# Sparse attention's pairs: the inverse of the sums on VectorE, narrow pairs in one bank, a later turn

## The reference, cut to what matters

```
p_sel = masked_softmax(q @ k_sel.T, pos <= t)
p_win = masked_softmax(q @ k_win.T, pos <= t)
o = gate0 * o_cmp + gate1 * (p_sel @ v_sel) + gate2 * (p_win @ v_win)
masked_softmax(s) = exp(s - max(s)) / sum(exp(s - max(s)))
```

## Time and profile before

| | |
|---|---|
| median of three runs | 1748.11 us |
| the profiled execution's own time | 1748.23 us |
| its span, first to last instruction | 1746.4 us |
| busy: PE / DVE / ACT / POOL | 98% / 56% / 47% / 55% of the span |
| the stage, first maximum to the last product of the values | 1034.1 to 1179.0 us, 8% of the span |

### The profile page before, as it was taken

The page is one execution under the profiler, slowest core; times in us unless marked ns, Lnnn a source line. Parts: engine busy times, 40 slices in busy tenths (PEclk is TensorE's granted clock), DMA queues, the critical chain, the costliest instruction groups (busy, mean ns, idle before and its releaser), DMA issues.

```text
span 1746.4 us, 27720 instructions
## 1 busy us (share of the span) xinstructions
PE 1712.6 (98%) x10482; PEld 1522.1 (87%) x10482; DVE 970.9 (56%) x1638; ACT 825.4 (47%) x1667; POOL 966.7 (55%) x703
## 2 busy tenths in 40 slices
PE   8999999999999999999999999999999999999998
PEld 6988887888888998999888978888988889989996
DVE  4345664244438871586058469984333498428832
ACT  4224553232335552455256358874533556426642
POOL 4544332235444874677446459982842468638862
PEclk9999999999999999999999999999999999999999
DMA  6422122123351433233435330012531223323331
GB/s 226 119 76 60 49 73 58 49 61 98 113 169 49 121 115 115 73 97 116 127 91 148 97 107 3 6 33 73 169 109 61 77 69 107 124 73 109 110 121 48
DMA packets 222902, 161.57 MB, mean 93 GB/s; under 512 B 9769, under 2 KB 197425, under 8 KB 222770
## 3 DMA queue, kind: packets, MB, share of 16 engines
q1 hardware_dynamic: 221712, 158.73, 30.4%
q10 hardware_dynamic: 1058, 1.07, 0.2%
HBM read 155.57 MB, written 2.11 MB: 90 GB/s over the span
## 4 chain that ended last, share of the span: by engine, by line
PE 86%; DVE 8%; issue 3%; ACT 2%; POOL 1%; DMA 0%; DVEq 0%; SPq 0%; ACTq 0%
PE psum L365 26%; PE psum L367 26%; PE psum L366 26%; DVE nprobL L2871 2%; DVE stat L2864 1%; PE psum L1172 1%; PE psum L451 1%; PE psum L2785 1%; DVE ffn_quarters L2071 1%; PE psum L1183 1%; DVE ffn_tl L2081 1%; PE psum L1195 1%; PE psum L1249 1%; PE psum L1231 0%; DVE oT L2882 0%
## 5 line engine op out<-in xcount | busy, mean ns | idle before, releaser
L352 POOL TENSOR_TENSOR w_low<-ring,w_high 128x1024 fp32r<-128x1024 f32 (+2 forms) x223 | 488.7, 2202 | 537.5 <-ACT w_high L344 537.1
L365 PE MATMUL psum<-hT,w_high 128*128 128x256 f32 (+1 forms) x1120 | 380.8, 340 | 0.0
L367 PE MATMUL psum<-hT,w_low 128*128 128x256 f32 (+1 forms) x1120 | 375.2, 335 | 0.0
L366 PE MATMUL psum<-hL,w_high 128*128 128x256 f32 (+1 forms) x1120 | 375.2, 335 | 0.0
L344 ACT ACTIVATE w_high<-ring 128x1024 fp32r<-128x1024 f32 (+2 forms) x223 | 211.3, 953 | 298.6 <-PE psum L367 288.4
L367 PEld LDWEIGHTS psum<-hT,w_low 128*128 128x128 f32 x1120 | 212.6, 190 | 22.0
L365 PEld LDWEIGHTS psum<-hT,w_high 128*128 128x128 f32 x1120 | 212.9, 190 | 19.5 <-DVE hL L470 0.2
L366 PEld LDWEIGHTS psum<-hL,w_high 128*128 128x128 f32 x1120 | 212.9, 190 | 19.1
L1840 POOL TENSOR_TENSOR w_low<-ffn_sums,w_high 128x512 fp32r<-128x512 f32 x120 | 164.1, 1381 | 75.0 <-ACT w_high L1835 74.9
L1840 POOL TENSOR_TENSOR w_low<-ring,w_high 128x512 fp32r<-128x512 f32 x120 | 164.6, 1383 | 47.5 <-ACT w_high L1835 46.0
L365 PE MATMUL psum<-ffn_th,w_high 128*128 128x256 f32 x640 | 182.4, 285 | 5.5 <-POOL w_low L1840 2.8
(11 more groups left out here) (447 smaller groups left out, 3723.4 us busy)
## 6 DMA issues: line engine op xcount, KB each, us to landing
ring<-in_w_in SPq DMA_DIRECT2D x58, 512.0 KB, 3.6
ring<-in_ffn_w_up SPq DMA_DIRECT2D x44, 512.0 KB, 3.8
ring<-in_w_gate SPq DMA_DIRECT2D x22, 512.0 KB, 3.8
ring<-in_w_up SPq DMA_DIRECT2D x22, 512.0 KB, 4.8
ring<-in_w_down SPq DMA_DIRECT2D x20, 512.0 KB, 4.0
ring<-in_ffn_w_down SPq DMA_DIRECT2D x20, 512.0 KB, 3.8
ring<-in_nsa_w_in SPq DMA_DIRECT2D x18, 512.0 KB, 3.6
ring<-in_ca_wkv SPq DMA_DIRECT2D x16, 512.0 KB, 3.7
```

The costliest lines, as they stand in the source:

```text
L352: nc.gpsimd.tensor_tensor(tile_view(w_low, n, SPLIT), tile_view(ring, n, RING), tile_view(w_high, n, SPLIT), ALU.subtract).then_inc(w_lo, 1)
L365: nc.tensor.matmul(ps, lhsT=sh, rhs=mh, start=first, stop=False)
L366: nc.tensor.matmul(ps, lhsT=sh, rhs=ml_, start=False, stop=False)
L367: return nc.tensor.matmul(ps, lhsT=sl, rhs=mh, start=False, stop=last)
```

## The change

Three edits, made together in this stage.

1. The inverse of the sums moves from POOL to DVE. POOL's line 2898 (with its wait and a constant of -1) goes. DVE computes `reciprocal` of pair s-1's two sums in step s, after the maximum of pair s and ahead of the leftovers. POOL's line 2900 now waits for DVE.
2. A *narrow* pair (t of 0 or 1: 128 or 256 columns a head) has both heads turned into one bank, 4 or 5 by turns. ACT copies both heads with one instruction and DVE subtracts both with one; the turn waits for the pair two before (`p_low` of 2p-2) and not for the one before. Wide pairs stay as they were. Where narrow and wide pairs meet, the turn waits for all of the pair before.
3. `turn(p)` is issued in step p+3 of PE rather than p+2; with it the copy and the leftovers go to step p+4, `values(p)` to step p+5, the additions to odd steps from 7 on, and the split of finished chunks one step later. The loops are one step longer.

```diff
--- before.py
+++ after.py
@@ -2750,7 +2750,21 @@
             g, t, hp, b = npairs[v_ // 2]
             return g, t, 4 * g + 2 * hp + v_ % 2, 4 * b + g
 
-        minus_one = stat[:, 36:38]
+        def in_one(p):
+
+            return npairs[p][1] <= 1
+
+        def turned_to(v_):
+            p, wd = v_ // 2, (npairs[v_ // 2][1] + 1) * P
+            return bank[4 + p % 2][:, v_ % 2 * wd:v_ % 2 * wd + wd] if in_one(p) else bank[4 + v_ % 2][:, 0:wd]
+
+        def turned_heads(p):
+
+            wd = (npairs[p][1] + 1) * P
+            at_ = 2 * (p % 2)
+            if in_one(p):
+                return [(2 * p + 1, bank[4 + p % 2][:, 0:2 * wd].rearrange("p (h c) -> p h c", c=wd), slice(at_, at_ + 2), wd)]
+            return [(v_, turned_to(v_), v_ % 4, wd) for v_ in (2 * p, 2 * p + 1)]
 
         def sum_of(o):
             return bank[6 + o % 2][:, 0:2 * P]
@@ -2779,11 +2793,19 @@
                 t = npairs[p][1]
                 for v_ in (2 * p, 2 * p + 1):
                     pe.wait_ge(p_scaled, v_ + 1)
-                    if v_ >= 2:
+                    if p >= 1 and in_one(p) != in_one(p - 1):
+                        pe.wait_ge(p_low, 2 * p)
+                    elif p >= 2 and in_one(p):
+                        pe.wait_ge(p_low, 2 * p - 2)
+                    elif p >= 1:
                         pe.wait_ge(p_low, v_ - 1)
+                    to = turned_to(v_)
                     for j in range(t + 1):
-                        mm = nc.tensor.transpose(bank[4 + v_ % 2][:, j * P:(j + 1) * P], nprob[:, v_ % 8, j * P:(j + 1) * P], ident)
-                    mm.then_inc(p_turned, 1)
+                        mm = nc.tensor.transpose(to[:, j * P:(j + 1) * P], nprob[:, v_ % 8, j * P:(j + 1) * P], ident)
+                    if not in_one(p):
+                        mm.then_inc(p_turned, 1)
+                if in_one(p):
+                    mm.then_inc(p_turned, 2)
 
             def values(p):
                 g, t, hp, b = npairs[p]
@@ -2807,13 +2829,13 @@
             scores(0)
 
             pe.wait_ge(c_done, 8)
-            for s in range(n_np + 4):
-                if s >= 4:
-                    values(s - 4)
+            for s in range(n_np + 5):
+                if s >= 5:
+                    values(s - 5)
                 if s + 1 < n_np:
                     scores(s + 1)
-                if 2 <= s < n_np + 2:
-                    turn(s - 2)
+                if 3 <= s < n_np + 3:
+                    turn(s - 3)
 
         def chunk_high(a, c):
             a.wait_ge(p_added, 8 * (c // 2) + 8)
@@ -2821,18 +2843,16 @@
 
         def chunks_at(s):
 
-            return [2 * (s // 16) - 2 + (s % 16 - 6) // 4] if s >= 16 and s % 16 in (6, 10) else []
+            return [2 * (s // 16) - 2 + (s % 16 - 7) // 4] if s >= 16 and s % 16 in (7, 11) else []
 
         @block.scalar
         def _(a):
-            for s in range(n_np + 3):
-                for v_ in ((2 * s - 6, 2 * s - 5) if s >= 3 else ()):
-                    t = npairs[v_ // 2][1]
+            for s in range(n_np + 4):
+                for v_, src, at_, wd in turned_heads(s - 4) if s >= 4 else ():
                     a.wait_ge(p_turned, v_ + 1)
-                    if v_ >= 4:
-                        a.wait_ge(p_summed, v_ // 2 - 1)
-                    nc.scalar.activation(nprobT[:, v_ % 4, 0:(t + 1) * P], bank[4 + v_ % 2][:, 0:(t + 1) * P],
-                                         ACT.Copy).then_inc(p_high, 1)
+                    if s >= 6:
+                        a.wait_ge(p_summed, s - 5)
+                    nc.scalar.activation(nprobT[:, at_, 0:wd], src, ACT.Copy).then_inc(p_high, 2 if in_one(s - 4) else 1)
                 if s < n_np:
                     wd = (npairs[s][1] + 1) * P
                     a.wait_ge(p_peaked, s + 1)
@@ -2855,7 +2875,7 @@
         @block.vector
         def _(v):
             link = Chain(v, p_chain)
-            for s in range(n_np + 6):
+            for s in range(n_np + 7):
                 if s < n_np:
                     wd = (npairs[s][1] + 1) * P
                     v.wait_ge(p_scored, s + 1)
@@ -2863,16 +2883,21 @@
                         v.wait_ge(p_exped, 2 * s - 2)
                     nc.vector.tensor_reduce(np_peak[s % 2], psum[:, 2 * (s % 2):2 * (s % 2) + 2, 0:wd], AXX,
                                             ALU.max, negate=True).then_inc(p_peaked, 1)
-                for v_ in ((2 * s - 6, 2 * s - 5) if 3 <= s < n_np + 3 else ()):
-                    t = npairs[v_ // 2][1]
+                if 1 <= s <= n_np:
+                    p = s - 1
+                    v.wait_ge(p_exped, 2 * p + 2)
+                    if p >= 2:
+                        v.wait_ge(p_scaled, 2 * p - 2)
+                    nc.vector.reciprocal(np_recip[p % 2], np_total[p % 3]).then_inc(p_inverted, 1)
+                for v_, src, at_, wd in turned_heads(s - 4) if 4 <= s < n_np + 4 else ():
                     v.wait_ge(p_high, v_ + 1)
-                    if v_ >= 4:
-                        v.wait_ge(p_summed, v_ // 2 - 1)
-                    nc.vector.tensor_tensor(nprobL[:, v_ % 4, 0:(t + 1) * P], bank[4 + v_ % 2][:, 0:(t + 1) * P],
-                                            nprobT[:, v_ % 4, 0:(t + 1) * P], ALU.subtract).then_inc(p_low, 1)
-                if s >= 6 and s % 2 == 0:
-
-                    o = (s - 6) // 2
+                    if s >= 6:
+                        v.wait_ge(p_summed, s - 5)
+                    nc.vector.tensor_tensor(nprobL[:, at_, 0:wd], src, nprobT[:, at_, 0:wd],
+                                            ALU.subtract).then_inc(p_low, 2 if in_one(s - 4) else 1)
+                if s >= 7 and s % 2 == 1:
+
+                    o = (s - 7) // 2
                     g, t, hp, _ = npairs[2 * o]
                     v.wait_ge(p_summed, 2 * o + 2)
                     if o == 0:
@@ -2887,16 +2912,11 @@
 
         @block.gpsimd
         def _(g_):
-            nc.gpsimd.memset(minus_one, -1.0).then_inc(zeroed, 1)
-            g_.wait_ge(zeroed, 3)
             for v_ in range(2 * n_np):
                 g, t, h, kb = unit_of(v_)
                 wd = (t + 1) * P
                 p, i = v_ // 2, v_ % 2
-                if i == 0:
-                    g_.wait_ge(p_exped, v_ + 2)
-                    nc.gpsimd.tensor_tensor(np_recip[p % 2], np_total[p % 3], minus_one, ALU.pow).then_inc(p_inverted, 1)
-                    g_.wait_ge(p_inverted, p + 1)
+                g_.wait_ge(p_inverted, p + 1)
                 nc.gpsimd.tensor_scalar(nprob[:, v_ % 8, 0:wd], nprob[:, v_ % 8, 0:wd], np_recip[p % 2][:, i:i + 1],
                                         gates[:, t, h, 1 + kb // 4:2 + kb // 4], ALU.mult, ALU.mult).then_inc(p_scaled, 1)
                 if v_ % 2 == 1:
```

## The result

The changed kernel takes 1751.86 us in the median of 20 runs (1747.66 to 1753.51), the kernel before 1748.76 us (1747.07 to 1751.42) in runs on the same chip. The ratio is 1.0016, 95% interval 1.0010 to 1.0023: 2.8 us slower (1.7 to 4.0; the two medians lie 3.10 apart). The ratio is inside the forecast range and inside the 0.2% that stand for no change, but its interval leaves out 1, so the kernel is a little slower by more than the scatter of the runs, and by 2 us more than the forecast sum of +0.9. Those 2 us hide larger errors of both signs.

The account below looks back on a forecast made before the run. The prediction took DVE's work plus waits to set the stage's length, with PE ruling the 128-wide stretch. Reciprocal +4.5, merge -2.2, changes of group -0.9, start -0.5 sum to +0.9 us on 1748.11: 1749.0 us, range 1744.5 to 1754.5.

Parts of the forecast that it names:

- I count the stage on DVE: Whole stage: its length is DVE's work plus DVE's waits; PE sets the pace only in the 128-wide stretch.
- The reciprocal: DVE's queue: 64 added reciprocals, each occupying 0.07 us, cost +4.5 us; upper end 12.2.
- PE soaks up the surplus: In the six of 16 steps that PE rules, extra DVE time costs nothing; used only in pricing a rival.
- The merge: Narrow pairs: both heads in one bank, one leftover for two on DVE, saves 2.2 us over 32 pairs.
- Each merge saves 0.07 us: DVE's narrow leftovers: one instruction of double width takes 0.07 us less than two.
- nothing, unless ACT were to fill up: ACT's merged copies: the time saved on ACT counts for nothing, as ACT has 5 us to spare a group.
- The later turn: Turn issued one step later: -0.9 us at the changes of group and -0.5 us at the stage's start.
- 0.3 for each change of group: Where one group's wide pairs meet the next's narrow ones: shorter DVE waits, -0.3 us at each of three changes.
- Work moved, not added: Stage's end: the longer pipeline loses nothing; pair 59 follows the last maximum first, the pace stays 2.16 us a pair.
- No overlap: Rival, chance 0.20: each reciprocal costs 0.19 us between maximum and leftovers on DVE, +4.8 us more, 1753.8 us.
- POOL was the bound: Rival, chance 0.20: waits in the narrow stretch and at the start are POOL's doing and go; -4.5 us, 1743.6 us.
- Held up by POOL: Rival, chance 0.05: POOL's instructions hold up DVE's reciprocals, as they do tiny copies (466 ns); +12 us, 1761 us.

Follow-up runs that it names:

- r_l: The changed kernel without the merge, heads in separate banks (reciprocal on DVE and later turn stay): ratio 1.0002 to the kernel before, stage 146.24 us.
- l_only: The kernel before with only the turn one step later; inverse on POOL, heads in separate banks: ratio 1.0005, stage 144.80 us.
- r_only: The kernel before with only the reciprocal moved to DVE; separate banks, turn at its old step: ratio 1.0003, stage 146.28 us.
- l_dummy: The kernel with the later turn alone, plus an unused reciprocal a pair on DVE, POOL's inverse kept: ratio 1.0007, stage 146.18 us.

## Why the prediction was right, and which of its steps were wrong

The time was right and the sum behind it was not: two terms were wrong by more than 3 us each, in opposite directions. That the sum came within 2 us of the result is luck.

- **What bounds the stage.** "I count the stage on DVE" was too simple. PE rules the 128-wide steps, as said (9.62 of 9.69 us), and DVE the 512-wide ones. But in the steps of 256- and 384-wide scores a loop through ACT rules, and work on DVE counts there in one step and is in part given back in the next: with the turn at its later step the eight reciprocals of these steps cost 0.10 us in all (r_l against l_only), with the turn at its old step 0.32 (r_only against before). The earlier trace rows held no wait of any size in these steps, and I took that for DVE being the bound; it was two engines just in time for each other.
- **The reciprocal**, +4.5 us: its price in the queue was right, 0.07 us (1079.87 to 1079.95), its length too. But it costs 1.4 us in all (stage: 1.38 from before to r_only, 1.44 from l_only to r_l, 1.38 from l_only to l_dummy). In steps in which PE or, with the later turn, the loop through ACT rules it mostly vanishes: r_l against l_only, step by step through a group, shows 0.06 or 0.07 in eight of 16 steps, 0.03 in two, and -0.06 in two steps with which the loop closes. I had written that PE soaks up the surplus under a rival, and left it out of the forecast's own sum.
- **The merge**, -2.2 us: wrong in sign, +2.1 to +2.5 us. "Each merge saves 0.07 us" held in steps without additions; the step that failed is the one that priced ACT's merged copies at "nothing, unless ACT were to fill up". ACT had time; what was not counted is that a merged leftover's first column waits for the last of the copy. By the fixed cost that the Trainium skill, "VectorE: DVE Perf Modes", section on the TRN2 errata, gives, each merge would have saved an estimated 0.125 us; the runs show 0.06 where it saves at all, and a loss of 2 us or more in the stage.
- **The later turn**, -1.4 us in all: -0.1. The two full groups gave 0.09 and 0.05 us where I had 0.3 for each change of group. The start gained more than the 0.5 I gave it (first maximum to that of pair 16: 30.94 us in l_only for 32.28) and the last group 0.7, and the tail took 2.09 back. "Work moved, not added" was right; but then the earlier maxima at the start are the same move, and no gain. The fifth maximum came 0.81 us earlier for a forecast 0.5.
- **The rivals.** No overlap: refuted by the pitch of 0.07 us. POOL was the bound: refuted by r_only and l_dummy. Held up by POOL: refuted, a mean of 157 ns beside a POOL that is busy 21.7 us a group; the split in the Trainium skill's "SBUF — State Buffer", section "Who interferes with whom", agrees with that number. None of them was the mechanism that decided. That the result is slower, as with no overlap, lends that rival nothing; its +5.7 us is also further from the measured +2.8 than the forecast's +0.9.
- **What was to show it.** Reciprocals near 0.155 us, leftovers of 0.42 and 0.69 us, POOL near 20 us a group and waits of the old kind of 1.3 us were all there; the group's 34.96 + 0.3 was not, and this row alone told of the error.

## What to carry to other kernels

Before merging two instructions into one, ask what the first of the two could start on: if its input is made by another engine just in time, the merged one starts a whole input later, and the saving of a fixed cost is small beside that. An engine without visible waits isn't thereby the bound: follow one result from engine to engine round to where it comes from, and compare the length of that loop with the engine's work. A deeper pipeline that gains at the start pays at the end, so look at the tail's own loop at the same time.

## What the runs showed that I had not expected

Fewer instructions on two engines, with less work on both, made the stage longer by over 2 us, and one wait for a second copy was worth 0.77 us a group, though the gaps that its trace lists for it are of 0.17 and 0.19 us: the two steps of the loop hand such a gap on to the next maximum. And taking a third of POOL's work away, 32.12 to 21.61 us in a group, changed the group by 0.02 us, although POOL had been as busy as DVE.
